# Two expert groups later: the order in which one core walks through its experts, and GpSimd's queue with it

## The reference, cut to what matters

```
t = h.reshape(512, 1024)                    # tokens after an RMS norm
glog = t @ w_rg + b_rg                      # 4 groups, the best one is taken
elog = t @ w_re + b_re                      # 16 experts, the best 2 of that group
combine[token, expert] = weight             # two nonzeros in each row
y = sum over e of combine[:, e] * (silu(t @ w_gate[e]) * (t @ w_up[e])) @ w_down[e]
out = rms_norm(x + y) * g_final
```

## Time and profile before

| | |
|---|---|
| time, median of 3 runs | 2105.56 us (2093.19 to 2112.1) |
| time of the profiled execution | 2101.65 us |
| its span | 2099.8 us |
| TensorE busy (share of span) | 2011.6 us (96%) |
| VectorE / ScalarE / GpSimd busy | 1265.8 us (60%) / 983.8 us (47%) / 136.8 us (7%) |
| HBM read / written | 307.12 MB / 32.51 MB |

### The profile page before, as it was taken

The page is one execution under the profiler, slowest core; times in us unless marked ns, Lnnn a source line. Parts: engine busy times, 40 slices in busy tenths (PEclk is TensorE's granted clock), DMA queues, the critical chain, the costliest instruction groups (busy, mean ns, idle before and its releaser), DMA issues.

```text
span 2099.8 us, 27981 instructions
## 1 busy us (share of the span) xinstructions
PE 2011.6 (96%) x10531; PEld 1594.7 (76%) x10531; DVE 1265.8 (60%) x2204; ACT 983.8 (47%) x1630; POOL 136.8 (7%) x238
## 2 busy tenths in 40 slices
PE   8999999999999999988999999999999999899995
PEld 7877788888888877768888888878778888635662
DVE  5575856585846356665757775747762546536753
ACT  4444545455434355544544553533562235125652
POOL 0000020000001000001000001102000000112101
PEclk9999999999999999999999999999999999899998
DMA  6234344542632243323435262462415516899898
GB/s 206 79 106 155 97 141 140 194 147 91 201 121 81 86 136 108 101 68 101 135 125 181 80 218 65 135 191 74 157 57 170 163 58 225 289 387 389 290 384 307
DMA packets 193854, 337.99 MB, mean 161 GB/s; under 512 B 15878, under 2 KB 103190, under 8 KB 193712
## 3 DMA queue, kind: packets, MB, share of 16 engines
q1 hardware_dynamic: 190096, 327.09, 45.8%
q0 software_dynamic: 3616, 9.03, 1.7%
HBM read 307.12 MB, written 32.51 MB: 162 GB/s over the span
## 4 chain that ended last, share of the span: by engine, by line
PE 81%; DVE 6%; DMA 4%; ACT 3%; POOL 2%; issue 2%; SPq 1%; DVEq 0%; ACTq 0%; POOLq 0%
PE ps L183 75%; PE ps L186 5%; POOL SM L218 2%; DVE WL L198 1%; SPq L223 1%; DMA RAW<-in_w_down_dram 1%; ACT WH L194 1%; ACT ST L194 1%; DMA XG<-hd,IDX 1%; POOL SM L215 1%; DVE X L208 1%; DMA ed<-ST 0%; DVE BR L198 0%; SPq L2791 0%; DVE JP L198 0%
## 5 line engine op out<-in xcount | busy, mean ns | idle before, releaser
L198 DVE TENSOR_TENSOR WL<-RAW,WH 128x1024 fp32r<-128x1024 f32 x394 | 475.3, 1222 | 253.6 <-ACT WH L194 250.8
L194 ACT ACTIVATE WH<-RAW 128x1024 fp32r<-128x1024 f32 x394 | 410.8, 1056 | 313.4 <-PE ps L183 192.5
L183 PE MATMUL ps<-XH,WH 128*128 128x512 f32 (+1 forms) x880 | 324.0, 368 | 3.7 <-DVE WL L198 3.7
L183 PE MATMUL ps<-XL,WH 128*128 128x512 f32 (+1 forms) x880 | 321.3, 365 | 0.0
L183 PE MATMUL ps<-XH,WL 128*128 128x512 f32 (+1 forms) x880 | 321.0, 365 | 0.0
L183 PE MATMUL ps<-WH,XH 128*128 128x512 f32 (+1 forms) x736 | 296.3, 403 | 0.8 <-ACT ST L194 0.8
L183 PE MATMUL ps<-WH,HR 128*128 128x512 f32 x928 | 289.0, 390 | 0.0
L183 PE MATMUL ps<-WH,XL 128*128 128x512 f32 (+1 forms) x736 | 284.4, 386 | 0.0
L183 PE MATMUL ps<-WL,XH 128*128 128x512 f32 (+1 forms) x736 | 283.7, 385 | 0.0
L183 PEld LDWEIGHTS ps<-WH,HR 128*128 128x128 f32 x928 | 174.2, 188 | 35.9
L183 PEld LDWEIGHTS ps<-XH,WH 128*128 128x128 f32 x880 | 168.5, 191 | 30.5 <-DVE WL L198 4.6
(11 more groups left out here) (368 smaller groups left out, 2835.6 us busy)
## 6 DMA issues: line engine op xcount, KB each, us to landing
RAW<-in_ffn_w_dram SPq DMA_DIRECT2D x164, 512.0 KB, 4.6
RAW<-in_w_down_dram SPq DMA_DIRECT2D x63, 512.0 KB, 13.1
RAW<-in_w_gate_dram SPq DMA_DIRECT2D x61, 512.0 KB, 10.8
RAW<-in_w_up_dram SPq DMA_DIRECT2D x57, 512.0 KB, 10.9
RAW<-in_w_in_dram SPq DMA_DIRECT2D x30, 512.0 KB, 4.4
RAW<-in_ev_w_in_dram SPq DMA_DIRECT2D x20, 512.0 KB, 4.6
RAW<-in_ple_w_gate_dram SPq DMA_DIRECT2D x16, 512.0 KB, 4.1
RAW<-in_od_w_in_dram SPq DMA_DIRECT2D x32, 256.0 KB, 3.4
```

The costliest lines, as they stand in the source:

```text
L183: return self.go(ns).matmul(o, lhsT=l, rhs=x, start=st, stop=sp)
L194: return self.go(0.83 * n + 55.0 + (130.0 if bias is not None else 0.0) + (100.0 if acc is not None else 0.0)).activation(o, i, f, scale=s ...
L198: return self.go(1.04 * n + 68.0).tensor_tensor(o, a, b, op)
```

## The change

Group (9, 11) moves behind groups 6 and 5. GpSimd's gathers follow `SLOTS`, and `SENDS` has new values for it.

```diff
@@ -564,10 +564,10 @@
     SHARED = {0: ((0, 0, 64), (1, 64, 64)), 1: ((2, 0, 32), (3, 32, 32), (4, 64, 32), (5, 96, 32)),
               2: ((6, 0, 32), (7, 32, 32), (8, 64, 32), (8, 96, 32))}
     PLACES = {i: sorted({p for p, _, _ in parts}) for i, parts in SHARED.items()}
-    GROUPS = ((0,), (2,), (8, 10), (7,), (9, 11), (6,), (5,), (4,), (3,), (1,))
+    GROUPS = ((0,), (2,), (8, 10), (7,), (6,), (5,), (9, 11), (4,), (3,), (1,))
     SLOTS = sum(GROUPS, ())
     LAST = SLOTS[-1]
-    SENDS = (0, 0, 0, 0, 1, 1, 2, 2, 4, 5, 7, 11)
+    SENDS = (0, 0, 0, 0, 1, 1, 2, 4, 5, 5, 6, 11)
```

## The result

| | before | after |
|---|---|---|
| median | 2103.0 us of 4 runs (2093.19 to 2112.1) | 2133.44 us of 4 runs (2123.49 to 2137.09) |
| profiled execution, span | 2101.65 us, 2099.8 us | 2132.87 us, 2131.1 us |

The ratio is 1.0138, with an interval of 1.0098 to 1.0178. The kernel became slower by 1.4%, some 29 us (the medians lie 30.4 us apart). The forecast was 2097 us with a range up to 2110.

A forecast was written before the change was run, and what follows sets the result against it. TensorE was taken to pace the groups and the weight stream the end; load 164 landing at 2033.8 plus 57.3 us gave 2091.1, a gain of 8.7 us. On the median: 2105.6 - 8.7 = 2096.9, taken as 2097, range 2086 to 2110.

The forecast's parts named there:

- behind no wait of their own: GpSimd's queue: g6 and g5 take the places of g9 and g11 with no wait of their own, cost put at nothing.
- SyncE's `count` waits for fan 5: SyncE's list: loads behind this wait, now about 1947 instead of 1987.7, are covered by 8 to 11 us of queued stream.
- I put both at nothing: GpSimd's new queue order and SyncE's wait for fan 5 were both priced at zero.
- planned right ahead of the fan: Start of fan (9,11): turns of slots 9 and 11 come just before it, a bubble of 0 to 3.3 us, taken as 2.
- the hole at load 120: Weight stream: load 120 issued only at 1958.77, after load 119 at 1946.95; the stream, full until 1958.6, could gain 8.7 us.
- Does the stall go: TensorE's 9.5 us stretch ahead of fan 6: 5.6 us can go, with slot 4's rows in place 27 us ahead.
- The stall only moves: Rival, chance 0.22: slot 4's turn again stands behind slot 11's, ahead of fan 4; gain only 4.6 us, 2101 us.
- Loads 148 to 151 ... have 4.6 us and more: Weight stream at fold (9,11), 1992.3 to 2004: these loads, due near 2009, have at least 4.6 us to spare.
- From there the end is a fixed piece: From load 164's landing to the end takes a fixed 57.3 us, so landing at 2033.8 gives an end of 2091.1.
- The slower rival: Chance 0.08: g11, behind slow transfers in GpSimd's queue, holds fan (9,11); at 14 us a transfer 8 us slower, 2113.6 us.
- over 40 us: Cost at fan (9,11) if each GpSimd transfer were as slow as a load, 18.9 us.
- Wrong if TensorE waits for gathered rows at fan (9,11) or fan 4: One of the stated signs in the changed profile, at these two TensorE stages, that would refute the forecast; no size given.

The follow-up runs named there:

- e1: Changed kernel with GpSimd's `count()` waiting for fan 4 instead of fan 5: median 2110.82 us, ratio 1.0051 to the kernel before.
- e2: Kernel before with GpSimd's `count()` waiting for fan (9,11) instead of fan 5: median 2107.36 us, ratio 1.0039 to the kernel before.
- e7: Changed kernel with GpSimd's `count()` on fan 4, g9 and g11 ahead of slot 2's scatters, g4 ahead of s7: 2106.43 us, ratio 1.0016 to before.
- e5: Changed kernel with the planner taking GpSimd's transfers to land 8 us after the end of their issue: 2098.75 us, ratio 0.9987 to before.
- e10: Changed kernel with GpSimd's landings planned at 8 us and g9 ahead of slot 2's scatters: 2099.44 us, ratio 0.9996 to before.
- e4: Kernel before with g6 ahead of slot 2's scatters: 2098.34 us, ratio 0.9988 to the kernel before.
- e6: Kernel before with the planner taking GpSimd's transfers to land 8 us after the end of their issue: 2100.44 us, ratio 0.9988 to before.
- e9: Kernel before with GpSimd's landings planned at 8 us and g6 ahead of slot 2's scatters: 2099.94 us, ratio 1.0001 to before.

## Why the prediction was wrong

**The step that failed: GpSimd's read.** The prediction says that g6 and g5 stand "behind no wait of their own" in GpSimd's queue, and of the wait for fan 5 only that "SyncE's `count` waits for fan 5"; "I put both at nothing". But `count()` stands on every engine, and on GpSimd it shares the list with `moves`. Its condition came 38 us forward (fan 5's end 1987.7 to 1949.6), and with it its place in the list. What stands behind the wait was asked for SyncE, where it held about 1 us, and not for GpSimd, the engine whose list the change rewrites. There the read held the third scatter of slot 2, g9, g11 and g4 for 38.8 us (the landing alone needed 7.0 before), and TensorE waited 21.2 us for their rows, a term that the sum has at nothing. Shown by e1 (taken out: 13.4 us of the stretch) and e2 (put in alone: 7.2 us).

**Second: the places of the turns.** The prediction has the turns of slots 9 and 11 "planned right ahead of the fan", and slot 4's ahead of fan 4. The planner put all three ahead of fold 6 or into it. For slot 4 that is one double group too early for where g4 stands. Price 8.4 us (e1), and e7, which moves g4 and the turns, is without it. It's the mirror of what the prediction read from the rows of before: a plan that takes landings at the wrong time misplaces turns, here too early against an issue that s7 holds back.

**The sum of the loss.** The stretch grew by 27.8 us. TensorE's idle time grew by 28.2 - 4.4 = 23.8 us, and its busy time for the same work by 166.8 - 162.9 = 3.9 us, at a mean clock of 0.91 for 0.98. Of the 27.8 us, taken away in this order, e1 puts 13.4 on the read, e7 10.5 on the gathers' places (171.2 for 181.7), and 3.9 are left (171.2 against 167.3). Of these, 3.6 are idle time of TensorE: e7 has waits of 3.52, 0.96, 0.66 and 2.88 us, all for VectorE, where before has 3.26, 0.65 and 0.34. In e5 the first two of them are absent.

**The gain was over-sized as well.** Forecast were 3.7 us in the stretch (fan 1 at 2026 for 2029.7) and 8.7 at the end. e5 and e10, where no turn waits for a gather, show 1.2 and 1.1 us in the stretch, and from the start of fan (8,10) to the end 237.3 us where before has 237.4. The base was high as well: the median of 2105.6 came from three runs, and later sets of 23 to 35 runs have 2099.7 to 2100.2. What held: fan 6 to fold 6 took 36.25 us for 36.3 forecast, fan (9,11) 20.85 for 20.9, and the hole at load 120 closed. What failed:
- "Does the stall go": from fold 5 to fan 1 the forecast has 49.4 us, e5 53.8. Of these 4.4 us 2.9 are a wait at a turn, behind slot 11's hidden rows ahead of fold (9,11), released by VectorE's write of EH; the rest goes with a clock of 0.94. So the stall moves, as the rival *The stall only moves* has it, but to another turn than the one named (slot 1's).
- "Loads 148 to 151 ... have 4.6 us and more": e5 has a hole of 11.5 us right there. A stream that runs ahead meets the double group's fold, which releases the loads only by use, and the hole at that fold is 6.0 us before, 8.9 in e4 and 11.5 in e5. Over the whole stretch the share was 0.98 before and 0.98 to 1.00 in e4, e5, e6, e9 and e10, where a full stretch has 1.03. The times were wrong too: by the prediction's own stages fold (9,11) ends 16.9 us ahead of 2024.1, at 2007.2 and not at 2004.
- "From there the end is a fixed piece", counted from load 164's landing. In e10 this load landed 10.6 us after fan 1's start, before 12.8 us, and the end came 60.5 us after the landing, before 57.3. From fan 1's start the rest took 69.2 to 72.1 us in all twelve kernels. The sum should have been the start of fan 1 plus 70: with the forecast's own 2026 the span ends at 2096, a gain of 3.7 us. Even that is a little too much, for in the five kernels with the shortest stretches (e4, e5, e6, e9, e10) the rest took 71.1 to 72.1 us.

**The slower rival** named the right engine and one of the right victims, g11, at 0.08. Its mechanism, slow transfers, is refuted: g9 took 9.2 us, and scatters that depend on each other went out 8.8, 10.1 and 9.6 us apart (before: 8.7 to 10.0). At 18.9 us a transfer its own sum ends at 2024.1 + 44.2 + 64.0 = 2132.3, 32.5 us slower (the "over 40 us" are fan (9,11)'s delay). That the measured span is 2131.1 is chance. "Wrong if TensorE waits for gathered rows at fan (9,11) or fan 4" was the right test, though the waits stood one stage earlier, ahead of fold 6 and in it.

**Left open.** Why fan (8,10) starts anywhere from 1857.3 to 1866.9 is not known, nor what s7 would do if ScalarE wrote fold 7's result earlier. By the ratio the whole loss is 29 us, by the spans 31.3, and by the stretch 27.8.

## What to carry to other kernels

When an order is changed, list every instruction on every engine that waits for the stage that moves, the small ones too: a register read that waits for it is pulled forward with it, and all DMAs behind it in that list wait as well. In the profile it has no row; it shows as a long idle time whose releaser (here a matmul) has no business with the instruction behind it. And before pricing a gain by a hole in the stream, look at the busier engine over the whole stretch: TensorE works for 162.9 of 167.3 us, so there were 4.4 us of idle time to take, and the best stretch of ten experiments, e4's, is 4.1 us shorter.

## What the runs showed of the hardware

A gather on GpSimd's queue landed 9.2 us after its issue while the DMA share was 1.03 (g9, at 1953.11), and 3.7 us after it when the stream had run dry (g11, at 1972.08). DMA: Bandwidth & Descriptors of the Trainium skill, Anatomy of one DMA (SWDGE path), gives about 2.0 us and the bytes at 436 GB/s; for 0.26 MB, the most that the 64 rows of g11 can be, that is an estimate of 2.6 us, and for a full slot 3.2 us. The trace is 1.1 us above the estimate for g11. A full slot, g4, landed 5.7 us after its issue at 1977.56, 2.5 us above. For a full stream the page has no figure, and the trace has three times the estimate. Issue to landing of g11, and the two stretches after the change:

```profile
DMA to landing us min/median/max: 3.7/3.7/3.7
```

```profile
1953.10:1964.00 10.90, 2.77 (x13) 2.38 (x13) 0.69 (x1) 2.35 (x4) 2.63 (x2) 0.50 1.03 392
1964.00:1988.80 24.80, 11.69 (x43) 9.03 (x42) 5.28 (x7) 5.77 (x9) 6.20 (x5) 0.60 0.44 96
```

Waiting costs more than its own length: after 23.8 us more of idle time TensorE needed 3.9 us more for the same matmuls, with a granted clock of 0.61 in the 39 us of the waits.
